# Moving the value products of latent attention between the two heads' turns

## What is computed

```python
def mla_attend(q_nope, q_pe, k_nope, k_pe, v, q_pos, k_pos):
    s = (einsum('bqhd,bkhd->bhqk', q_nope, k_nope)
         + einsum('bqhr,bkr->bhqk', q_pe, k_pe)) * MLA_SCALE
    visible = (k_pos[None, :] // CHUNK) <= (q_pos[:, None] // CHUNK)
    p = softmax(where(visible, s, -inf))
    return einsum('bhqk,bkhd->bqhd', p, v)

def stick_breaking_attend(q, k, v, q_pos, k_pos):
    z = einsum('bqhd,bkhd->bhqk', q, k) * SB_SCALE
    log_keep = where(before, log_sigmoid(-z), 0)
    between = cumsum(log_keep, reverse) - log_keep
    return einsum('bhqk,bkhd->bqhd', where(before, exp(log_sigmoid(z) + between), 0), v)
```

## Time and profile before

| | |
|---|---|
| median of 3 runs | 1703.98 us (1703.95 to 1706.08) |
| the profiled execution, its own time | 1708.17 us |
| its span | 1706.4 us |
| PE busy in the span | 1677.7 us (98%) |
| DVE, ACT, POOL busy | 1067.1, 529.3 and 500.1 us |
| the MLA and sample steps (10 to 33) in the span | 376 to 578 us |

### The profile page before, as it was taken

One profiled execution on the slowest core, in us unless ns is written; L12 is line 12 of the kernel. 1 busy time (PEld: TensorE's weight loads), 2 busy tenths in 40 slices (PEclk: granted clock), 3 DMA queues, 4 the chain that ended last, 5 costly groups with the idle time before them and its releaser, 6 DMA issues.

```text
span 1706.4 us, 26499 instructions
## 1 busy us (share of the span) xinstructions
PE 1677.7 (98%) x10487; PEld 1546.5 (91%) x10487; DVE 1067.1 (63%) x1440; ACT 529.3 (31%) x955; POOL 500.1 (29%) x231
## 2 busy tenths in 40 slices
PE   9999999999999999999999999999999999999998
PEld 8899889776667699998999999999999999999997
DVE  7483477896657655437677656565655656565566
ACT  7220122586566441115332130211203021120222
POOL 2683042000000114330234343333433333343332
PEclk9999999999999999999999999999999999999999
DMA  5322121330212214316211111111111111111113
GB/s 206 92 85 81 57 64 36 109 87 12 97 65 82 99 59 145 118 38 265 90 38 42 46 37 49 37 49 37 39 47 37 49 37 45 41 37 49 38 47 112
DMA packets 36333, 119.41 MB, mean 70 GB/s; under 512 B 6048, under 2 KB 9344, under 8 KB 33952
## 3 DMA queue, kind: packets, MB, share of 16 engines
q1 hardware_dynamic: 33952, 108.89, 19.8%
q10 hardware_dynamic: 2304, 9.44, 1.6%
HBM read 100.86 MB, written 15.17 MB: 68 GB/s over the span
## 4 chain that ended last, share of the span: by engine, by line
PE 92%; DVE 4%; ACT 2%; issue 1%; POOL 1%; DMA 0%; SPq 0%; DVEq 0%; ACTq 0%; POOLq 0%
PE scores L2097 35%; PE bank L2097 35%; PE scores L2402 3%; PE bank L2459 3%; PE scores L2193 2%; PE bank L2483 2%; PE bank L2106 1%; PE scores L2115 1%; PE scores L2424 1%; PE bank L2513 1%; PE bank L2517 1%; PE bank L2476 1%; PE bank L2754 1%; DVE kbuf L1740 1%; ACT m_prob L1352 1%
## 5 line engine op out<-in xcount | busy, mean ns | idle before, releaser
L916 POOL TENSOR_TENSOR w_hi<-w_raw,zero 128x1024 fp32r<-128x1024 f32 x96 | 187.4, 1952 | 1111.3 <-PE bank L2097 466.2
L2097 PE MATMUL scores<-act_hi,w_hi 128*128 128x384 f32 x920 | 310.2, 337 | 0.9 <-POOL w_lo L919 0.9
L2097 PE MATMUL scores<-act_lo,w_hi 128*128 128x384 f32 x920 | 309.1, 336 | 0.0
L2097 PE MATMUL scores<-act_hi,w_lo 128*128 128x384 f32 x920 | 309.1, 336 | 0.0
L919 POOL TENSOR_TENSOR w_lo<-w_raw,w_hi 128x1024 fp32r<-128x1024 f32 x96 | 252.6, 2631 | 7.5
L2025 DVE TENSOR_TENSOR x<-bank,x 128x384 f32<-128x384 f32 x216 | 120.5, 558 | 103.5 <-PE bank L2097 103.5
L2097 PE MATMUL bank<-act_hi,w_hi 128*128 128x384 f32 x544 | 183.8, 338 | 0.9 <-POOL w_lo L919 0.9
L2097 PE MATMUL bank<-act_hi,w_lo 128*128 128x384 f32 x544 | 182.8, 336 | 0.0
L2097 PE MATMUL bank<-act_lo,w_hi 128*128 128x384 f32 x544 | 182.8, 336 | 0.0
L2097 PEld LDWEIGHTS scores<-act_hi,w_hi 128*128 128x128 f32 x920 | 173.0, 188 | 2.5 <-POOL w_lo L919 1.5
L2097 PEld LDWEIGHTS scores<-act_lo,w_hi 128*128 128x128 f32 x920 | 173.0, 188 | 0.0
(11 more groups left out here) (398 smaller groups left out, 3112.2 us busy)
## 6 DMA issues: line engine op xcount, KB each, us to landing
w_raw<-wstream SPq DMA_DIRECT2D x106, 512.0 KB, 3.6
x_blk<-xT ACTq DMA_DIRECT2D x8, 576.0 KB, 4.6
x_mid<-x_blk ACTq DMA_DIRECT2D x8, 576.0 KB, 3.1
x<-x_mid SPq DMA_DIRECT2D x4, 1152.0 KB, 5.2
z<-cache_k SPq DMA_DIRECT2D x4, 1024.0 KB, 5.3
z<-cache_v SPq DMA_DIRECT2D x4, 1024.0 KB, 7.3
mk_c<-mk_c SPq DMA_DIRECT2D x4, 1024.0 KB, 11.6
mv_c<-mv_c SPq DMA_DIRECT2D x4, 1024.0 KB, 13.6
```

The lines of the kernel that those rows point to most:

```text
L916: pool.tensor_tensor(w_hi[:, k], w_raw[:, k], zero[:].unsqueeze(2).to_broadcast([P, KB, P]), ALU.add).then_inc(w_rounded, 1)
L2097: mm = pe.matmul(out, w[:, k, at + kb], x(kb), start=first and kb == 0 and n == 0, stop=last and kb == n_kb - 1 and n == 2)
```

## The change

Only PE's program changes. In every round from step 10 to step 33, `values(t - 2)` moves from behind head 1's transposes and slot 1 to a place behind head 0's transposes and slot 0, ahead of `scores(t, 1)`. In the two last rounds (t = 34 and 35) the order stays.

```diff
@@ in the loop on t of PE's program
             for t in range(N_SB, N_STEPS + 2):
                 for hh in range(2):
...
                     if t <= N_STEPS and hh < n_heads(t - 1):
                         transposes(t - 1, hh)
                     for chunk in STEP_CHUNKS[t][hh]:
                         project_chunk(*chunk)
-                if STEPS[t - 3][0] == "sbs":
-                    pe.wait_ge(sb_picked, STEPS[t - 3][1] + 1)
+                    if hh == 0 and t < N_STEPS:
+                        if STEPS[t - 3][0] == "sbs":
+                            pe.wait_ge(sb_picked, STEPS[t - 3][1] + 1)
+                        values(t - 2)
                 if t >= N_STEPS:
+                    if STEPS[t - 3][0] == "sbs":
+                        pe.wait_ge(sb_picked, STEPS[t - 3][1] + 1)
                     latent_scores(t - N_STEPS)
-                values(t - 2)
+                    values(t - 2)
                 for chunk in STEP_CHUNKS[t][2]:
                     project_chunk(*chunk)
```

## The result

| | before | after |
|---|---|---|
| median of 5 runs each, on the same chip | 1704.61 us (1703.95 to 1707.52) | 1730.56 us (1730.32 to 1730.76) |
| ratio, with its 95% interval | | 1.0147 (1.0135 to 1.0159) |
| first scores of step 10 to first latent scores ("the stage") | 196.16 us | 224.05 us |
| from there to the first matmul of the output projection ("behind it") | 35.89 us | 31.11 us |

A forecast was written before the change was run, and what follows sets the result against it. PE, busy 98% of the span, was taken as the bound; 18.3 + 5.5 - 0.9 = 22.9 us, plus 6.8 for the clock, 29.7 on 1708.17, gave 1737.9, less 4.2 for the median: 1733.7 us, range 1721 to 1746.

The forecast's parts named there:

- Slot 2 behind query chunks: Nine steps where slot 2 follows slot 1's query chunk: PE waits for DVE's query copy, about 1.4 to 1.9 us each.
- Key chunks: Steps 11, 18 and 24: slot 2 waits for ACT's key copy, 1.36 us each, 4.1 in all.
- Shorter distances: Steps 10, 15, 16, 23, 28, 30 to 33 and round 34: less work ahead of waiting matmuls, 5.5 us lost.
- Step 15's gain: Step 15's 0.88 us wait for ACT's copy vanishes, as sample value products now stand before it: -0.9 us.
- Sample steps costed at nothing: Steps 13, 17, 21, 25: waits, 1.3 us in all, vanish but return at the end of the sample's DVE and ACT chain.
- The sum at an unchanged clock: Whole change without clock drops: 18.3 for slot 2, plus 5.5 for shorter distances, less 0.9 in step 15: 22.9 us.
- rival 5: Bank 7 free before PE comes: slot 2 loses nothing, 3.8 us of waits could go, 1700.2 us; chance 0.04.
- The clock: Pauses of steps 14, 19, 20, 26, 27: two of five followed by a drop of 3.4 us, 6.8 in all.
- Rival 2: Slot 2's pauses come but the clock stays full: 1726.9 us; chance 0.27.
- the forecast: Pauses in the MLA and sample steps with one to three clock drops: 1733.7 us, case range 1730 to 1737; chance 0.45.
- Rival 3: Clock falls behind most slot 2 pauses: five drops give 1743.9 us, all twelve 1768; chance 0.19.
- Rival 4: Slot 2's pauses real but smaller, DVE reaching the query copy earlier, nine gaps of 0.6 us: 1717 us; chance 0.05.

The follow-up runs named there:

- e6: Changed kernel, with slot 1's query copy on DVE put directly behind head 1's maximum, ahead of finish and group copy; 1720.24 us, ratio 1.0091 to the kernel before.
- e5: Kernel before, with the value products still behind head 1's transposes but ahead of slot 1 in place of behind it; 1717.51 us, ratio 1.0075.
- e4: Kernel before, with the value products moved in step 15 alone; 1705.91 against 1705.88 us, ratio 0.9996.
- e1: Kernel before, with the value products moved only in the twelve steps with chunks in slots 1 and 2; 1732.47 against 1704.89 us, ratio 1.0158.
- e3: Kernel before, with the value products moved only in sample steps 13, 17, 21 and 25; 1706.17 against 1704.59 us, ratio 1.0001.
- e10: Kernel before, with e9's early sigmoid and e3's move of the value products together; 1701.38 us, ratio 0.9974.
- e7: Kernel before, with values and slot 1 ahead of head 1's scores in ten steps, slot 1's copy taken first on DVE and ACT; 1713.04 us, ratio 1.0049.
- e9: Kernel before, with one tiny sigmoid on ACT starting each sample step, so the table load runs early; 1701.42 against 1704.59 us, ratio 0.9978.
- e8: Kernel before, with GpSimd's splitting of the output weights behind the MLA steps started one item later; 1704.82 against 1705.88 us, ratio 0.9998.

## Why the prediction was right, step by step

- **Slot 2 behind query chunks**: predicted 15.15, measured 14.7 in the totals, 14.8 one by one. Steps 19, 20 and 27: 1.76, 1.87 and 1.86 for 1.85. Steps 14 and 26: 1.90 and 2.05 for 1.9. Step 12: 1.53 for 1.6. Steps 10, 16 and 23: 1.10, 1.35 and 1.35 for the estimated 1.4. That DVE's sequence moves along with PE was the step that carried it, and 3.81 after is 3.81 before. e6 and e5 show its two parts.
- **Key chunks**: 1.36 each predicted, 1.29 measured three times.
- **Shorter distances**: 5.5 predicted, 2.8 measured, so half of this term was wrong. Step 16 has 0.46 for 0.6, step 33 has 0.90 for 0.8 + 0.3, round 34 has 0.69 + 0.54 for 1.7. Step 28 and steps 10, 15 and 23 show no wait for 1.2 predicted: ACT's output copy and pick-up were there in time. Step 30 has 0.21 for 0.3, and steps 31 and 32 show none for 0.6.
- **Step 15's gain**: 0.9 predicted. The wait is gone in the full change, but alone the move pays nothing (e4), and in e1 the wait goes without it. The prediction called it gained without asking what DVE does next. That it holds in the sum is owed to the longer pauses of steps 14 and 16.
- **Sample steps costed at nothing**: shown. The four waits of 0.34 went. In place of the old 0.40, 0.39 and 0.85 stand 0.39, 0.81, 0.40, 1.26 and 0.40 (e3: stage unchanged), and the move pays 1.56 when the chain is shorter (e10).
- **The sum at an unchanged clock**, 22.9: the stage grew by 27.9 less 3.4, so 24.5. The listed waits give less. They are 24.7 after (added one by one) and were 4.8 before, so they grew by 19.9, three below the sum. (Before is 4.8 and not the 3.8 of rival 5: that sum takes three of the view's six entries.) The rest, 4.6 us, is what each pause costs beyond its idle time (19.9 against 17.4 in e1, 11.4 against 8.7 in e5), and nearly all of it stands in PE's busy time, which grew in the stage by 7.7 us, 3.4 of them the slower clock. The prediction had no such term. That it made up for the distances that did not come is luck.
- **The clock**: the mis-sized term. Two drops were predicted and two came, but each cost 1.7 us, not 3.4. The price was read from the one profiled execution of before, and there it was at its highest: behind the same two pauses of 1.42 and 1.22 the lower level lasted 6.8 us in before, e1 and e3, and 3.4 us, half as long, in e4, e5, e7, e9 and e10. So the pairing of the pauses does not set the price; what does stays open. The number of two was a choice between none and five and not worked out. 6.8 predicted, 3.4 measured.
- **Not foreseen**: behind the stage the pause of 1.42 and the drop went, by the new order of round 34. The drop is in only some of the executions of before. The 58 in the experiments fall in three groups: 30 from 1704.01 to 1704.93 us, 19 from 1705.47 to 1706.89, and 9 from 1707.50 to 1708.20, at mean granted clocks of 0.998 or 0.999, 0.997 or 0.998, and 0.996. The groups are about 1.7 us apart, as if by no drop, a short one and a long one; traces of the kernels with the old round 34 show the last two (e4 at 1706.04, before at 1708.17). The median of before in the result, 1704.61, lies in the first group. So only the 1.4 of the pause counts in the difference of medians. 24.5 + 3.4 - 1.4 = 26.5, and 25.95 was measured.

So the mechanism was right: the waits, who releases them and how long they are. That the total fits to 3.1 us owes something to luck, as the errors have both signs: too high by 2.7 for the distances, 3.4 for the clock and 1.4 behind the stage, too low by 4.6 for what a pause costs beyond its idle time.

Rival 2, the pauses at full clock (1726.9), and the forecast (1733.7) lie 3.7 below and 3.1 above the result: its cause is the forecast's, pauses with two drops, and its price lies between. Rival 3 fell: two drops in twelve pauses. The section of the Trainium skill cited there ("HAM oscillation — how this bites in real kernels" on the page "TensorE: Matmul & The Clock Gate") describes waits longer than these, so that each of the twelve pauses would cost a drop did not follow from it; here ten of twelve pauses of 1.10 to 2.05 us were not followed by one. Rival 4, smaller pauses, and rival 5, bank 7 free in time, fell on DVE's unchanged 3.81; e6 made rival 4's case by an edit, and landed at 1720.24.

What stays open: why of the pauses of 1.76 us and more some are followed by a drop and others are not. The longest in the stage (step 26) is not among the two of after, but is among the three of e1, and 1.92 in e7 and 2.10 in e8 were followed by none.

## What to carry to other kernels

On an engine that hardly ever waits, a block of work is also a cover: before it is moved, list which buffers are freed and which chains run while it executes, and read from the other engines' rows how long they need from the event that starts them. Here the single bank that two engines hand to and fro needed work between its uses that does not need it. A short gain (0.88 us, four times 0.34) can be given back to the chain behind it. Where that chain was shortened first (e9), the same move paid (e10). And a price read from one execution may be that execution's own: look at the spread of the others before it goes into a sum.

## What the runs showed of the hardware

- A single pause of 1.53 us or less in the stage was never followed by a lower granted clock (seven such slot 2 pauses each in after and e1, twelve each in e5 and e6). Of twelve pauses of 1.76 to 2.10 us (five in after, five in e1, one each in e7 and e8) five were, at about 1.7 us each.
- The same two pauses of 1.42 and 1.22 us were followed by the lower level for 6.8 us in three traces and for 3.4 us in five.
- DVE's scaling of 128 x 640 took 0.55 us, or 2.43 and 2.60 when a GpSimd operation had begun 0.27 and 0.10 us earlier. A shift of some 0.4 us between the two, made by the order of PE's work in round 34, took a pause of 1.42 us from PE.
- Twelve pauses of TensorE cost 2.5 to 2.7 us more than their listed idle time, at the same matmuls and with the clock taken out.
